# Sliding-window attention in rounds between the projections' blocks, stick-breaking attention one head per round

## The chip, the cores and the metric

One core of a Trainium2 chip runs the whole program. The metric is the device time of one execution in microseconds; the lower the better.

## What is computed

Two blocks on 512 tokens of width 1024. The first (gated delta net, differential attention, two SwiGLU layers) is not touched. In the second block the first mixer, `swa_sb_mixer`, projects the normalised rows into five parts: queries for 8 heads of 64 (qa), keys and values of 2 heads (ka, va), and queries, keys and values of 8 heads (qb, kb, vb).

- Sliding-window attention on qa, ka, va: q and k get an RMS norm and a rotation by position; each block of 128 queries sees its own 128 keys and the 128 before it, and a mask leaves the last 128 keys of each query. With s the scaled scores and a learned sink per head, m = max(max s, sink) and p = exp(s - m) / (sum exp(s - m) + exp(sink - m)); the output is p times va.
- Stick-breaking attention on qb, kb, vb: z = q k / 8 for the keys before the query; the weight of a key is exp(logsigmoid(z) - sum of softplus(z) over the keys between it and the query).

Both outputs side by side (1024 wide) are multiplied by `w_out` and added to x. Cross-attention to 256 memory rows, a convolutional FFN and a second layer follow.

## The kernel before, in words

Five programs, one per engine, are written out in full (`pe_program`, `act_program`, `dve_program`, `pool_program`, `sp_program`), and the order on an engine is the order in which its program issues. Each engine counts its instructions in one semaphore; a helper's `sig` gives an instruction a key, and `wait_ge(*K.at(key))` on another engine waits for it. `meet` (line 194) is a barrier of TensorE, VectorE, ScalarE and GpSimd. `bank` (line 213) hands out the eight PSUM banks in turn and waits until the former holder of a bank was read; `free` notes those reads.

Weights come in tiles of up to 2048 words. SyncE loads tile t once tile t - 2 was split; ScalarE makes the high part (fp32r), VectorE the low part, both inside `tile` (lines 352 and 314), one tile ahead of its use; TensorE waits for the low part. A projection multiplies with three fp32r matmuls for each product (`mm3`, line 232: lines 233, 234, 235). `mm` (line 229) is a plain matmul, here f32, `tr` (line 237) a transpose through the identity. In the trace an f32 `mm` leaves two records, an fp32r one or a `tr` one.

The stage that the change touches:

- `pe_ab_proj` (line 2505): projections of qa, of ka and va together, of qb, kb and vb, two weight tiles each. qa, ka/va and vb come out by tokens (`pe_proj_tok`, line 716: four banks are held over both tiles, 12 matmuls of each bank per tile), qb and kb by features (`pe_proj_feat`, line 699: one bank of 24 matmuls per 128 features). ScalarE copies the results out of PSUM; VectorE norms and rotates q and k in four steps (`dve_rotate`, line 2581), each with a square root on ScalarE in its middle. Last, 24 transposes turn q, k and a swapped copy of k.
- A barrier. Then sixteen sliding units, `SW_UNITS` (line 2628): block of 128 queries times a pair of heads, four in flight, started in turn by `pipeline` (line 404). Per unit: TensorE makes the scores; VectorE adds the mask, takes the maximum and subtracts it; ScalarE takes the exp; VectorE sums; TensorE transposes p (four transposes; two in block 0, which has no block before it), ScalarE copies it, TensorE makes the output, VectorE scales it (`pe_sw_unit`, `act_sw_unit`, `dve_sw_unit`, lines 2636 to 2714).
- A barrier. Then the eight heads of stick-breaking, two in flight (lines 2722 to 2808). Per head: scores in four banks (512, 384, 256 and 128 columns), scaled into z by VectorE; ScalarE takes abs, exp and ln of 1280 columns, with a table load ahead of ln and of the next exp; VectorE adds max(z, 0); GpSimd masks the four diagonal blocks; TensorE sums over the keys with a triangle and ones (`sb_after`); VectorE subtracts; ScalarE takes the exp; GpSimd masks again; TensorE makes the output; VectorE copies it. Both heads wait for the two before them.
- A barrier. Then eight turns of four transposes each give the output projection its features (`pe_ab_to_feat`, line 2811, with `act_to_feat` and `dve_to_feat` for the high and low parts), and `pe_cross` begins with that projection. GpSimd loads the memory rows here (`pool_cross_loads`).

Of the kernel before, what the change touches and what calls it, by code (L numbers as in the profile page):

```python
# [698 lines left out]
def pe_proj_feat(p, K, tag, src, hT, segs, ready=None):  # L699
    for c0 in range(0, src.shape[1], 256):  # L700
        m = p.tile((0, src[:, c0:c0 + 256]))
        w = K.wview(m, 256, 8)
        for f in range(2):
            for s, (o, n) in enumerate(segs):
                key = (tag, c0 // 128 + f, s)
                b = p.bank(*key)
                for k in range(8):
                    if ready and c0 + f + s == 0:
                        p.wait_ge(*K.at(*ready, k))
                    ins = p.mm3(b[:, 0:n], [x[:, k, f * 128:(f + 1) * 128] for x in w], [x[:, k, o:o + n] for x in hT],  # L710
                                k == 0, k == 7)
                ins.then_inc(*p.sig(key, ("used", m)))
                p.close(*key)


def pe_proj_tok(p, K, tag, src, hT, tiles, ready=None):
    n = src.shape[1]
    bs = [p.bank(tag, t) for t in tiles]
    for kh in range(2):
# [12 lines left out]
        if not kh:  # L732
            ins.then_inc(*p.sig(("used", m)))
# [1697 lines left out]


def act_to_feat(a, K, tag):
    for n, k, o, w in feat_order(4):
        a.wait_ge(*K.at(tag, n))
        a.cp(K.H5[0][:, k, :], K.ps(tag, n)[:, :]).then_inc(*a.sig((tag + "_hi", n)))


def dve_to_feat(v, K, tag):
    for n, k, o, w in feat_order(4):  # L2440
        v.wait_ge(*K.at(tag + "_hi", n))
        v.lo([x[:, k, :] for x in K.H5], K.ps(tag, n)[:, :]).then_inc(*v.sig((tag + "_lo", k)))
        v.free(tag, n)


# [46 lines left out]
def swapped_k(K):  # L2492
    return K.mem(SWW + 1600, 512).rearrange("p (t n) -> p t n", n=128)
# [10 lines left out]

def pe_ab_proj(p, K):
# [5 lines left out]
    pe_proj_feat(p, K, "ab_kb", wi[:, 1280:1792], K.H5, [(0, 512)])  # L2511
    pe_proj_tok(p, K, "ab_vb", wi[:, 1792:2304], K.H5, t4)
# [7 lines left out]


def act_ab_proj(a, K):
    qk, q5, k5, va, qb5, kb5, vb = ab_mem(K)
    cs, gr, snk, posi, posf, ang, kk, sn, co = ab_small(K)
    a.tile()
    a.tile()
    for i, dst in enumerate((sn, co)):
# [11 lines left out]
    for tag, dst, t0 in (("ab_qb", qb5, 0), ("ab_kb", kb5, 2)):  # L2539
        for j in range(2):  # L2540
            a.tile()
            for f in (2 * j, 2 * j + 1):
                a.wait_ge(*K.at(tag, f, 0))
                a.cp(dst[:, f, :], K.ps(tag, f, 0)[:, :]).then_inc(*a.sig())
                a.free(tag, f, 0)
            a.root(K.tmpc[:, 60:70], ("ab", t0 + j))
    a.tile()
    a.tile()
    for t in range(4):
        a.wait_ge(*K.at("ab_vb", t))  # L2550
        a.cp(vb[:, t, :], K.ps("ab_vb", t)[:, :]).then_inc(*a.sig())
        a.free("ab_vb", t)
# [53 lines left out]
def dve_ab_proj(v, K):  # L2606
# [3 lines left out]
    dve_angles(v, K)  # L2610
    dve_tok_out(v, K, "ab_q", range(4), lambda t: qk[:, t, 0:512])
    v.tile()
    v.tile()
    for t in range(4):
        v.tile()
        dve_rotate(v, K, t)
    v.tile()
    v.tile()
# [3 lines left out]
    for k in range(1, 6, 2):  # L2622
        v.wait_ge(*K.at("ab_T", k))
        v.cp(q5[:, k, :] if k < 4 else k5[:, k - 4, :], K.ps("ab_T", k)[:, :]).then_inc(*v.sig())
        v.free("ab_T", k)

# [4 lines left out]
def sw_mem(K, n):  # L2631
    j = n % 4
    return K.mem(SWW + 1600 + j * 1024, 512), K.mem(SWW + 2112 + j * 1024, 512), K.tmpc[:, j * 16:j * 16 + 16]


def pe_sw_unit(p, K, n, blk, hp):
    qk, q5, k5, va, qb5, kb5, vb = ab_mem(K)
    s, pt, c = sw_mem(K, n)
    size = 256 if blk else 128
    nb = size // 128  # L2640
    b = p.bank("sw_s", n)
    for u in range(2):
        h = hp + 2 * u
        half = h % 2
        kT, pr = k5[:, 0 if h // 4 == half else 1, :], slice(half * 64, half * 64 + 64)
        ins = p.mm(b[:, u * size:(u + 1) * size], q5[pr, h // 2, blk * 128:(blk + 1) * 128],
                   kT[pr, (blk + 1) * 128 - size:(blk + 1) * 128])
    ins.then_inc(*p.sig(("sw_s", n)))
    p.close("sw_s", n)
    yield  # L2650
    yield
    s3 = s[:, 0:2 * size].rearrange("p (u n) -> p u n", u=2)
    p.wait_ge(*K.at("sw_e", n))
    b = p.bank("sw_T", n)
    for u in range(2):
        for k in range(nb):
            ins = p.tr(b[:, (u * nb + k) * 128:(u * nb + k + 1) * 128], s3[:, u, k * 128:(k + 1) * 128])
    ins.then_inc(*p.sig(("sw_T", n)))
    p.close("sw_T", n)
    yield  # L2660
    p.wait_ge(*K.at("sw_p", n))
    b = p.bank("sw_o", n)
    for u in range(2):
        g = (hp + 2 * u) // 4
        for k in range(nb):
            ins = p.mm(b[:, u * 64:u * 64 + 64], pt[:, (u * nb + k) * 128:(u * nb + k + 1) * 128],
                       va[:, blk - nb + 1 + k, g * 64:g * 64 + 64], k == 0, k == nb - 1)
    ins.then_inc(*p.sig(("sw_o", n)))
    p.close("sw_o", n)


def act_sw_unit(a, K, n, blk, hp):
    s, pt, c = sw_mem(K, n)
    size = 256 if blk else 128
    s3 = s[:, 0:2 * size].rearrange("p (u n) -> p u n", u=2)
    yield
    a.wait_ge(*K.at("sw_d", n))
    a.act(s3, s3, ACT.Exp).then_inc(*a.sig())
    a.act(c[:, 2:4], c[:, 2:4], ACT.Exp).then_inc(*a.sig(("sw_e", n)))
    yield  # L2680
    a.wait_ge(*K.at("sw_T", n))
    if n >= 4:
        a.wait_ge(*K.at("sw_o", n - 4))
    a.cp(pt[:, 0:2 * size], K.ps("sw_T", n)[:, 0:2 * size]).then_inc(*a.sig(("sw_p", n)))
    a.free("sw_T", n)
    yield


def dve_sw_unit(v, K, n, blk, hp):
    cs, gr, snk = ab_small(K)[0:3]  # L2690
    s, pt, c = sw_mem(K, n)
    size = 256 if blk else 128
    s3 = s[:, 0:2 * size].rearrange("p (u n) -> p u n", u=2)
# [1522 lines left out]
```

## Time and profile before

| | |
|---|---|
| median of 3 runs | 4329.79 us (4325.04 to 4331.91) |
| the profiled execution, its time | 4329.3 us |
| its span, first to last instruction | 4327.5 us |
| mean granted TensorE clock | 0.937 |
| TensorE matmul busy | 3916.8 us, 91% |
| TensorE weight load busy | 3240.4 us, 75% |
| VectorE busy | 2124.9 us, 49% |
| ScalarE busy | 1587.7 us, 37% |
| GpSimd busy | 588.5 us, 14% |
| chain of waits, share of TensorE | 77% |

All times are of one profiled execution, from its first instruction on. The granted clock is a share of full speed: 1.00 is 2.4 GHz, 0.50 is 1.2 GHz. Matmuls overlap, so what one adds is the distance between starts and not the duration of one. A busy share says nothing of how fast the engine ran while busy.

### The profile page before, as it was taken

What the parts mean: (1) busy time and instruction counts of PE and PEld (TensorE: products, weight loads), DVE (VectorE), ACT (ScalarE), POOL (GpSimd) and SP (SyncE); (2) the same over time, 40 slices, a digit from 0 to 9 for tenths busy, and PEclk for the clock granted to TensorE, in tenths of its full rate; (3) what the DMA queues carried; (4) which work ended last, traced back from release to release, by engine and by line L of the source; (5) the groups of instructions that cost most, each with busy time, mean ns of one, the idle gap of its engine ahead of it and who ended that gap; (6) DMA issues with size and microseconds to landing.
All of it is one profiled execution on the core that took longest, in us unless ns stands there. A gap on an engine that the chain in (4) does not pass through costs nothing.

```text
span 4327.5 us, 67031 instructions
## 1 busy us (share of the span) xinstructions
PE 3916.8 (91%) x28034; PEld 3240.4 (75%) x28034; DVE 2124.9 (49%) x3061; ACT 1587.7 (37%) x2550; POOL 588.5 (14%) x692
## 2 busy tenths in 40 slices
PE   6988897878999988988899798898999998889999
PEld 4866786766888766856788586677888787677887
DVE  3545554656121453277423656454555427545564
ACT  3333333333111332164323334544334336544333
POOL 0035303532000001002100000200120003000220
PEclk8988898888999999999899895999999999899999
DMA  4234433131111121103122320141323230322322
GB/s 153 81 129 145 143 95 116 35 106 56 62 63 65 54 80 59 59 1 109 59 98 93 73 93 1 33 136 40 97 95 102 83 112 17 102 86 69 98 98 88
DMA packets 248532, 355.04 MB, mean 82 GB/s; under 512 B 9299, under 2 KB 158502, under 8 KB 247846
## 3 DMA queue, kind: packets, MB, share of 16 engines
q1 hardware_dynamic: 233840, 300.49, 21.5%
q0 software_dynamic: 13840, 50.11, 3.7%
q8 instruction: 220, 3.60, 0.4%
q14 instruction: 82, 0.67, 0.0%
q10 hardware_dynamic: 550, 0.17, 0.0%
HBM read 336.50 MB, written 14.24 MB: 81 GB/s over the span
## 4 chain that ended last, share of the span: by engine, by line
PE 77%; DVE 11%; ACT 6%; POOL 2%; issue 2%; DMA 1%; ACTq 0%; DVEq 0%; SPq 0%; POOLq 0%
PE psum L233 20%; PE psum L235 20%; PE psum L234 20%; PE psum L230 13%; ACT arena L341 3%; PE psum L239 3%; DVE arena L264 3%; DVE arena L274 2%; DVE rx L335 2%; POOL arena L379 1%; DVE rw L264 1%; DVE arena L278 1%; ACT arena L345 1%; ACT rw L345 1%; DVE arena L270 1%
## 5 line engine op out<-in xcount | busy, mean ns | idle before, releaser
L233 PE MATMUL psum<-rx,rw 128*128 128x512 f32 (+2 forms) x2768 | 1026.3, 371 | 47.0 <-DVE rx L335 29.1
L234 PE MATMUL psum<-rx,rw 128*128 128x512 f32 (+2 forms) x2768 | 1011.1, 365 | 0.0
L235 PE MATMUL psum<-rx,rw 128*128 128x512 f32 (+2 forms) x2768 | 1010.4, 365 | 0.0
L230 PE MATMUL psum<-arena 32*32 32x32 f32 (+10 forms) x13078 | 833.3, 260 | 173.7 <-ACT arena L345 59.7
L264 DVE TENSOR_TENSOR rw<-arena,rw 128x2048 fp32r<-128x2048 f32 (+2 forms) x239 | 538.5, 2253 | 862.5 <-ACT rw L345 857.4
L230 PEld LDWEIGHTS psum<-arena 32*32 32x32 f32 (+5 forms) x13078 | 649.1, 144 | 339.0 <-issue 108.4
L345 ACT ACTIVATE rw<-arena 128x2048 fp32r<-128x2048 f32 (+2 forms) x239 | 448.2, 1875 | 802.5 <-PE psum L235 780.6
L233 PE MATMUL psum<-rw,rx 128*128 128x512 f32 (+1 forms) x1720 | 676.7, 393 | 36.8 <-DVE rx L335 27.6
L234 PE MATMUL psum<-rw,rx 128*128 128x512 f32 (+1 forms) x1720 | 670.5, 390 | 0.0
L235 PE MATMUL psum<-rw,rx 128*128 128x512 f32 (+1 forms) x1720 | 670.3, 390 | 0.0
L233 PEld LDWEIGHTS psum<-rx,rw 128*128 128x128 f32 (+1 forms) x2768 | 530.8, 192 | 144.9 <-DVE rx L335 41.3
L379 POOL TENSOR_TENSOR arena<-arena 128x512 f32<-128x512 f32 (+5 forms) x364 | 446.7, 1227 | 1228.5 <-DVE arena L274 628.5
L345 ACT ACTIVATE arena<-psum 128x512 f32<-128x512 f32 (+6 forms) x675 | 313.9, 465 | 790.5 <-PE psum L235 438.5
L234 PEld LDWEIGHTS psum<-rx,rw 128*128 128x128 f32 (+1 forms) x2768 | 531.4, 192 | 84.2 <-issue 4.1
L235 PEld LDWEIGHTS psum<-rx,rw 128*128 128x128 f32 (+1 forms) x2768 | 530.7, 192 | 82.1 <-issue 0.3
L341 ACT ACTIVATE arena<-arena 128x512 f32<-128x512 f32 (+10 forms) x492 | 258.7, 526 | 501.1 <-DVE arena L274 219.8
L233 PEld LDWEIGHTS psum<-rw,rx 128*128 128x128 f32 x1720 | 325.4, 189 | 113.2 <-DVE rx L335 36.4
L274 DVE SCALAR_TENSOR_TENSOR arena<-arena 128x512 f32<-128x512 f32 (+7 forms) x465 | 351.9, 757 | 56.6 <-ACT arena L341 40.6
L235 PEld LDWEIGHTS psum<-rw,rx 128*128 128x128 f32 x1720 | 325.6, 189 | 67.4
L234 PEld LDWEIGHTS psum<-rw,rx 128*128 128x128 f32 x1720 | 325.8, 189 | 64.6
L239 PE MATMUL psum<-arena 128*128 128x128 f32 (+2 forms) x1300 | 212.9, 310 | 141.6 <-DVE arena L269 45.3
L264 DVE TENSOR_TENSOR arena<-arena,psum 128x512 f32<-128x512 f32 (+4 forms) x316 | 153.1, 484 | 308.6 <-PE psum L235 201.1
(71 smaller groups left out, 2068.7 us busy)
## 6 DMA issues: line engine op xcount, KB each, us to landing
arena<-in_ffn_w_up SPq DMA_DIRECT2D x66, 1024.0 KB, 5.1
arena<-in_ada_w SPq DMA_DIRECT2D x48, 1024.0 KB, 5.2
arena<-in_ffn_w_down SPq DMA_DIRECT2D x40, 1024.0 KB, 5.1
arena<-in_ffn_w_gate SPq DMA_DIRECT2D x22, 1024.0 KB, 5.1
arena<-in_dn_w_in SPq DMA_DIRECT2D x32, 512.0 KB, 5.3
arena<-in_xa_w_kv SPq DMA_DIRECT2D x16, 1024.0 KB, 5.0
arena<-in_hgrn_w_in SPq DMA_DIRECT2D x16, 1024.0 KB, 5.5
arena<-in_da_w_in SPq DMA_DIRECT2D x12, 1024.0 KB, 5.2
```

The source lines that it names most:

```text
L230: return self.e.matmul(out, l, r, start=start, stop=stop)
L233: self.e.matmul(out, l[0], r[0], start=start, stop=False)
L234: self.e.matmul(out, l[0], r[1], start=False, stop=False)
L235: return self.e.matmul(out, l[1], r[0], start=False, stop=stop)
L239: return self.e.transpose(out, a, self.K.ident[0:k, 0:k])
L264: return self.e.tensor_tensor(out, a, b, op)
L270: return self.e.tensor_scalar(out, a, s1, s2, op0, op1)
L274: return self.e.scalar_tensor_tensor(out=out, in0=a, scalar=s, in1=b, op0=op0, op1=op1)
L335: return self.e.tensor_tensor(dst[1], src, dst[0].bitcast(F32), SUB)
L341: return self.e.activation(out, a, f, **kw)
L345: return self.e.activation(out, a, ACT.Copy, **kw)
L379: return self.e.tensor_tensor(out, a, b, op)
```

## The change

- The sliding units are no longer a stage. `pe_proj_feat` and `pe_proj_tok` get a call `behind` after each block, and TensorE, ScalarE and VectorE go through 18 rounds: two behind each of the four kb blocks, one behind each of the eight half blocks of vb, two at the end. Round i has the scores of unit i, the output of unit i - 2 and the transposes of unit i - 1.
- The 24 transposes of q and k move from behind the vb projection to before the kb projection.
- The mask is added in PSUM by TensorE: a second, fp32r matmul of the identity with the mask, both copied once by ScalarE. The exp reads PSUM, with scale, with the negated maximum as its bias, and with its sum taken on the way; VectorE only takes the maximum and small columns.
- On ScalarE the square root of a rotation step comes before the eviction of the block, on VectorE two rotations follow each other between splits.
- Stick-breaking runs in ten rounds of one head, with z in four places and the softplus in two. Round i has the sums of head i - 1, the scores of head i + 1 and the output of head i - 2.
- The eight turns of the output are put into these rounds (rounds 1 to 4, 4, 6, 8 and 9).
- The three barriers go; GpSimd waits for the last head's output before it loads the memory rows.

```diff
-def pe_proj_feat(p, K, tag, src, hT, segs, ready=None):
+def pe_proj_feat(p, K, tag, src, hT, segs, ready=None, behind=None):
...
+            if behind:
+                behind(c0 // 128 + f)
...
 def pe_ab_proj(p, K):
...
     pe_proj_feat(p, K, "ab_qb", wi[:, 768:1280], K.H5, [(0, 512)])
-    pe_proj_feat(p, K, "ab_kb", wi[:, 1280:1792], K.H5, [(0, 512)])
-    pe_proj_tok(p, K, "ab_vb", wi[:, 1792:2304], K.H5, t4)
     p.wait_ge(*K.at("ab_ksw"))
     for k in range(6):
...
+    def behind(f):
+        for i in (2 * f, 2 * f + 1):
+            pe_sw(p, K, i)
+
+    pe_proj_feat(p, K, "ab_kb", wi[:, 1280:1792], K.H5, [(0, 512)], None, behind)
+    pe_proj_tok(p, K, "ab_vb", wi[:, 1792:2304], K.H5, t4, None, lambda kh, t: pe_sw(p, K, 8 + kh * 4 + t))
+    for i in (16, 17):
+        pe_sw(p, K, i)
...
 def dve_ab_proj(v, K):
...
     for t in range(4):
-        v.tile()
+        if t % 2 == 0:
+            v.tile()
         dve_rotate(v, K, t)
...
+    for i in range(18):
+        if i in (0, 4, 8, 12):
+            v.tile()
+        dve_sw(v, K, i)
...
+def pe_sw(p, K, i):
...
+            p.mm(b[:, u * size:(u + 1) * size], q5[pr, h // 2, blk * 128:(blk + 1) * 128],
+                 kT[pr, (blk + 1) * 128 - size:(blk + 1) * 128], True, False)
+            ins = p.mm(b[:, u * size:(u + 1) * size], one, mask[:, 256 - size:256], False, True)
+        ins.then_inc(*p.sig(("sw_s", i)))
+        p.close("sw_s", i)
+    if sw_unit(i - 2):
+        blk, hp = sw_unit(i - 2)
+        pt, nb = sw_mem(K, i - 2)[1], sw_size(i - 2) // 128
+        p.wait_ge(*K.at("sw_p", i - 2))
+        b = p.bank("sw_o", i - 2)
...
+    if sw_unit(i - 1):
+        e = sw_mem(K, i - 1)[0]
+        p.wait_ge(*K.at("sw_e", i - 1))
+        b = p.bank("sw_T", i - 1)
...
+def act_sw(a, K, i):
+    if sw_unit(i):
...
+            a.act(e[:, u * size:(u + 1) * size], K.ps("sw_s", i)[:, u * size:(u + 1) * size], ACT.Exp, scale=0.125,
+                  bias=bias[:, u:u + 1], accum_out=total[:, u:u + 1]).then_inc(*a.sig(("sw_e", i)))
+        a.free("sw_s", i)
+        a.act(sink, sink, ACT.Exp).then_inc(*a.sig(("sw_sum", i)))
+    if sw_unit(i - 1):
+        pt, n = sw_mem(K, i - 1)[1], 2 * sw_size(i - 1)
+        a.wait_ge(*K.at("sw_T", i - 1))
...
+        a.cp(pt[:, 0:n], K.ps("sw_T", i - 1)[:, 0:n]).then_inc(*a.sig(("sw_p", i - 1)))
...
+def dve_sw(v, K, i):
...
+        v.red(bias, r2(K.ps("sw_s", i)[:, 0:2 * sw_size(i)], 2), MAX).then_inc(*v.sig())
+        v.stt(bias, bias, -0.125, sinks(K)[:, hp:hp + 3:2], MUL, MIN).then_inc(*v.sig())
+        v.tt(sink, snk[:, hp:hp + 3:2], bias, ADD).then_inc(*v.sig(("sw_d", i)))
...
+def pe_sb(p, K):
...
+    sb_scores(p, K, 0)
+    for i in SB_ROUNDS:
+        if 0 <= i - 1 < 8:
+            h = i - 1
+            sp = sb_mem(K, h)[1]
+            p.wait_ge(*K.at("sb_fail", h))
...
+        if i + 1 < 8:
+            sb_scores(p, K, i + 1)
+        if 0 <= i - 2 < 8:
+            h = i - 2
+            z = sb_mem(K, h)[0]
+            p.wait_ge(*K.at("sb_a", h))
...
+        for k in sb_turns(i):
+            pe_ab_turn(p, K, k)
+
+def sb_turns(i):
+    return [k for k in range(8) if i == (k + 1 if k < 4 else min(2 * k - 4, 9))]
...
+def act_sb(a, K):
+    for i in SB_ROUNDS:
...
+            a.act(sp, sp, ACT.Ln, bias=1.0).then_inc(*a.sig(("sb_ln", i)))
+        if 0 <= i - 1 < 8:
+            z = sb_mem(K, i - 1)[0]
+            a.wait_ge(*K.at("sb_loga", i - 1))
+            a.act(z, z, ACT.Exp).then_inc(*a.sig(("sb_exp", i - 1)))
+        for k in sb_turns(i):
+            act_ab_hi(a, K, k)
...
+def pool_sb(g, K):
...
+            g.wait_ge(*K.at("sb_exp", i - 1))
+            for c0, size in CB:
+                g.tt(z[:, c0:c0 + 128], z[:, c0:c0 + 128], usm, MUL).then_inc(*g.sig(("sb_a", i - 1)))
+        if i < 8:
+            sp = sb_mem(K, i)[1]
+            g.wait_ge(*K.at("sb_sp", i))
+            for c0, size in CB:
+                g.tt(sp[:, c0:c0 + 128], sp[:, c0:c0 + 128], usm, MUL).then_inc(*g.sig(("sb_fail", i)))
...
+def pe_ab_turn(p, K, k):
+    if k < 4:
+        p.wait_ge(*K.at("sw_out", 15))
+    else:
+        p.wait_ge(*K.at("sb_out", 2 * k - 7))
...
     pe_ab_proj(p, K)
-    p.meet("ab_proj")
-    pipeline([pe_sw_unit(p, K, n, *u) for n, u in enumerate(SW_UNITS)], 4)
-    p.meet("sw")
-    pipeline([pe_sb_unit(p, K, h) for h in range(8)], 2)
-    p.meet("sb")
-    pe_ab_to_feat(p, K)
+    pe_sb(p, K)
...
     pool_ab_loads(g, K)
-    g.meet("ab_proj")
-    g.meet("sw")
-    pipeline([pool_sb_unit(g, K, h) for h in range(8)], 2)
-    g.meet("sb")
+    pool_sb(g, K)
+    g.wait_ge(*K.at("sb_o", 7))
     pool_cross_loads(g, K, 0)
```

## Rows read from the trace of the kernel before

**Rows 1.** Busy time by stretch: length, TensorE, weight load, VectorE, ScalarE, GpSimd, clock, DMA, GB/s
```profile
2600.00:2650.00 50.00, 49.72 (x165) 38.38 (x164) 41.04 (x105) 16.10 (x36) 0.00 (x0) 0.50 0.00 1
```

**Rows 2.** Chain of waits, 2440 to 2850: start us, us, engine, line, count
```profile
2483.93 5.34 PE psum L239 x32
...
2588.21 2.63 PE psum L239 x24
...
2617.65 1.04 PE psum L239 x4
2618.70 3.60 PE psum L230 x12
...
2661.93 5.24 PE psum L230 x8
...
2773.01 5.87 PE psum L239 x32
```

**Rows 3.** VectorE in order of time, the rotations and their surroundings
```profile
2527.89 0.82 DVE L264 TENSOR_TENSOR arena<-arena 128x640 f32<-128x640 f32 x1
...
2543.58 0.82 DVE L264 TENSOR_TENSOR arena<-arena 128x640 f32<-128x640 f32 x1
...
2550.95 2.29 DVE L264 TENSOR_TENSOR rw<-arena,rw 128x2048 fp32r<-128x2048 f32 x1
...
2581.69 0.62 DVE L290 COPY arena<-arena 128x256 f32<-128x256 f32 x2
```

**Rows 4.** ScalarE in order of time, the last eviction of qb
```profile
2544.72 0.60 ACT L345 ACTIVATE arena<-psum 128x512 f32<-128x512 f32 x1 [4.84 <-PE psum L235]
```

**Rows 5.** Busy time by stretches of 4 us, columns as in rows 1
```profile
2484.00:2488.00 4.00, 4.00 (x22) 4.00 (x23) 1.91 (x3) 2.50 (x4) 0.00 (x0) 0.58 0.74 25
...
2512.00:2516.00 4.00, 4.00 (x35) 4.00 (x35) 1.34 (x2) 0.53 (x1) 0.00 (x0) 1.00 0.24 65
...
2592.00:2596.00 4.00, 0.77 (x10) 0.57 (x8) 3.14 (x10) 1.15 (x1) 0.00 (x0) 1.00 0.00 0
...
2604.00:2608.00 4.00, 4.00 (x13) 2.96 (x12) 3.48 (x10) 1.00 (x3) 0.00 (x0) 0.50 0.00 0
...
2692.00:2696.00 4.00, 4.00 (x27) 3.28 (x26) 1.71 (x5) 2.39 (x2) 0.01 (x1) 1.00 0.00 0
...
2712.00:2716.00 4.00, 4.00 (x32) 3.83 (x31) 1.59 (x5) 1.27 (x1) 1.06 (x3) 1.00 0.00 0
```

**Rows 6.** Groups by shape in 2592 to 2662: busy us, mean ns, idle before
```profile
L278 DVE TENSOR_REDUCE arena<-arena 128x2 f32<-128x512 f32 x24 | 16.5, 686 | 1.7
...
L345 ACT ACTIVATE arena<-psum 128x512 f32<-128x512 f32 x12 | 7.2, 597 | 1.5 <-PE psum L239 0.5
...
L341 ACT ACTIVATE arena<-arena 128x256 f32<-128x256 f32 x4 | 1.7, 417 | 5.1 <-DVE arena L264 5.0
...
L341 ACT ACT_TABLE_LOAD x1 | 1.3, 1283 | 3.8 <-DVE arena L264 3.8
```

**Rows 7.** The four engines' orders of time in stick-breaking, 2660 to 2775
```profile
2676.20 21.05 PE L230 MATMUL psum<-arena 128*128 128x512 f32 x96 [6.49 <-POOL arena L379]
...
2684.27 1.27 ACT L341 ACTIVATE arena<-arena 128x1280 f32<-128x1280 f32 x1 [4.08 <-DVE arena L264]
...
2705.31 1.49 DVE L274 SCALAR_TENSOR_TENSOR arena<-arena 128x1280 f32<-128x1280 f32 x1 [5.05 <-ACT arena L341]
...
2716.87 2.29 DVE L269 TENSOR_SCALAR arena<-psum 128x512 f32<-128x512 f32 x4 [0.63 <-PE psum L230]
...
2758.41 2.05 POOL L379 TENSOR_TENSOR arena<-arena 128x128 f32<-128x128 f32 x4 [4.49 <-DVE arena L274]
...
2760.52 6.78 PE L230 MATMUL psum<-arena 128*128 128x512 f32 x40 [0.46 <-POOL arena L379]
...
2765.78 1.27 ACT L341 ACTIVATE arena<-arena 128x1280 f32<-128x1280 f32 x1 [3.78 <-DVE arena L264]
...
2769.23 3.26 PE L230 MATMUL psum<-arena 128*128 128x64 f32 x20 [1.93 <-POOL arena L379]
```

More of the change, by code:

```diff
@@ L713, in pe_proj_feat, with pe_proj_tok @@
                 p.close(*key)
-def pe_proj_tok(p, K, tag, src, hT, tiles, ready=None):
+            if behind:
+                behind(c0 // 128 + f)
+def pe_proj_tok(p, K, tag, src, hT, tiles, ready=None, behind=None):
     n = src.shape[1]
@@ L731, in pe_proj_tok @@
                 p.close(tag, t)
-        if not kh:
-            ins.then_inc(*p.sig(("used", m)))
+            elif t == tiles[-1]:
+                ins.then_inc(*p.sig(("used", m)))
+            if behind:
+                behind(kh, t)
 def out_chunks(Kn):
@@ L2538, in act_ab_proj @@
         a.free("ab_k", t)
-    for tag, dst, t0 in (("ab_qb", qb5, 0), ("ab_kb", kb5, 2)):
-        for j in range(2):
+    for f in range(4):
+        if f % 2 == 0:
             a.tile()
[L2542 to L2552, printed above, removed]
+        a.root(K.tmpc[:, 60:70], ("ab", f))
+        feat("ab_qb", qb5, f)
     for k in range(0, 6, 2):
         a.wait_ge(*K.at("ab_T", k))
-        a.cp(q5[:, k, :] if k < 4 else k5[:, k - 4, :], K.ps("ab_T", k)[:, :]).then_inc(*a.sig())
+        a.cp(q5[:, k, :] if k < 4 else k5[:, k - 4, :], K.ps("ab_T", k)[:, :]).then_inc(*a.sig("ab_T_a"))
         a.free("ab_T", k)
+    for f in range(4):
+        if f % 2 == 0:
+            a.tile()
+        feat("ab_kb", kb5, f)
+        for i in (2 * f, 2 * f + 1):
+            act_sw(a, K, i)
+    for kh in range(2):
+        a.tile()
+        for t in range(4):
+            if kh:
+                a.wait_ge(*K.at("ab_vb", t))
+                a.cp(vb[:, t, :], K.ps("ab_vb", t)[:, :]).then_inc(*a.sig("ab_vb_out"))
+                a.free("ab_vb", t)
+            act_sw(a, K, 8 + kh * 4 + t)
+    for i in (16, 17):
+        act_sw(a, K, i)
 def dve_angles(v, K):
@@ L2631, in sw_mem, with sinks, sw_mask @@
+def sinks(K):
+    return K.tmpc[:, 72:80]
+def sw_mask(K):
+    return K.rx[:, 8192:8320], K.rx[:, 8320:8576]
 def sw_mem(K, n):
     j = n % 4
-    return K.mem(SWW + 1600 + j * 1024, 512), K.mem(SWW + 2112 + j * 1024, 512), K.tmpc[:, j * 16:j * 16 + 16]
-def pe_sw_unit(p, K, n, blk, hp):
-    qk, q5, k5, va, qb5, kb5, vb = ab_mem(K)
[L2638 to L2669, printed above, removed]
```

279 lines of the change are left out of this document (140 added, 139 removed).

## The prediction

> **What bounds the kernel now.** The busy shares say that TensorE works 91% of the span, and the same holds in the two stages that the change touches, so I read its clock next. In the 50 us table one stretch of these stages has TensorE busy 49.72 of 50 us at a granted clock of 0.50 [rows 1]: full, and at half speed. The chain of waits [rows 2] gives the borders. The last projection ends at 2588.2; 24 transposes of q and k follow (2.63 us, 0.11 each, at full clock); the sixteen sliding units run until stick-breaking begins at 2661.93; the eight turns run from 2773.01 for 5.87 us, to 2778.88. A full unit (12 of 16) is 4 transposes and 12 matmul records, 1.04 + 3.60 = 4.64 us, back to back, on TensorE itself. An f32 matmul leaves two records, an fp32r one or a transpose one. The clock fell because TensorE did almost nothing in 2592 to 2596, and 13 records in 4 us did not raise it again [rows 5]. So sinking the units beside projections hides nothing from TensorE: both are its work. What it can win is the clock and gaps. Stick-breaking is different: TensorE waits there for POOL, and the next two heads cannot start before both heads are out.
>
> **Part 1, the projections.** The transposes move ahead of the kb projection, so they wait for the rotated q and k, which VectorE makes. Before, kb and vb covered that. The last qb eviction starts at 2544.72 [rows 4], so qb ends at 2544.65. On VectorE rotation 0 starts at 2527.89; rotation 1 starts at 2543.58 and the next operation at 2550.95, so a rotation without a stall is 7.3 us [rows 3]. The square root no longer stands behind an eviction, so all four take this: 4 x 7.3 = 29.2, one weight split 2.29 + 0.05 between them, and the swapped copies 0.7 [rows 3]. That gives 2527.89 + 32.2 = 2560.1. TensorE stands from 2544.65 to 2560.1, **15.5 us idle that is new**. ScalarE's order is no bound: its splits need only earlier weight tiles used. The negated sinks and the two mask copies lie before these waits beside the q projection and cost nothing; without that cover under 1 us.
>
> After such a gap the transposes start cold. In 2484 to 2488 a run of 32 transposes after a long idle had a mean clock of 0.58 [rows 5], and all 32 took 5.34 us [rows 2]: the rise came 3.4 us in. For 24 I take 3.4 us at 0.23 and 9 at 0.11, 4.4 us. The Trainium skill, page "TensorE: Matmul & The Clock Gate", Part 4, states that the clock gate does not open for transposes; here it opened inside a run of nothing else, so the measurement decides. By that rule the 24 would cost 6.2 us and the sum below come out 1.8 us later.
>
> Dense work left, kb and vb: 2588.2 - 2544.65 = 43.5 us.
>
> The sunk units: with no long idle beside them I take them at the full level. That the clock holds over such work is seen in 2692 to 2696 and 2712 to 2716, when only stick-breaking's half-height scores and 64-column outputs ran, at 1.00 [rows 5]. A full unit is half of 4.64, 2.3 us; the second of these windows gives 0.125 per record, 8 output records 1.0 us, which agrees. The mask adds two fp32r matmuls of 256 columns; the k projection has this shape, 35 in 4 us [rows 5], 0.11 each, so 0.23. 12 x 2.55 = 30.6; the four block-0 units have half of most of it, about 1.4, 5.6 together. **36 us.** Switching between f32 and fp32r inside one sum is seen nowhere; I take nothing, and a whole extra fp32r matmul (0.11) for each of 32 mask matmuls, 3.5 us, as the upper end.
>
> Waits in the rounds: between a unit's scores and its transposes lie the reduction 0.69 [rows 6], two small operations, two exps of 0.42 each (256 columns) and between that and the outputs a copy of 0.60 behind the next unit's exps [rows 6]. That is 2.9 us from scores to copied; TensorE has 2.2 to 2.5 us of its own between them in the two back-to-back rounds of a kb block, so 0.75 us is open in each of three blocks and 1.3 in the first; with a vb block of 2.7 us between rounds nothing is open; the two tail rounds leave 1.5 and 0.75. Sum 5.5. VectorE's own addition of the mask and subtraction of the maximum go as well; TensorE was the one waited for in nearly all full units, so this is counted at nothing. For clock dips I add 2 us.
>
> New end: 2560.1 + 4.4 + 43.5 + 36 + 5.5 + 2 = 2651.6, before 2661.9: **10.3 us won**.
>
> **Part 2, stick-breaking.** Follow one head per round. In round i POOL first masks the outputs of head i-1 (after its last exp), then the softplus of head i; TensorE sums head i after both; VectorE subtracts; ScalarE takes the exp. That is a loop: exp of head i-1, POOL 2.05, POOL 2.05, TensorE's sums to exp start 5.26 (2760.52 to 2765.78, warm), exp 1.27 [rows 7], hand-overs 0.25: 10.9 us. Beside it, ScalarE's three passes and two table loads (1.28 each [rows 6]) reach the exp's table load at 10 us in rounds with a turn, so 11 us. VectorE has 2.29 for the next scores, 1.49 for the softplus [rows 7], as much as 2.3 for the subtractions and a small copy, 6.5 us; TensorE 4.5 + 2.2 + 2.2 to 2.5 + a turn of 0.45, 9.4 us: neither is the bound while warm. TensorE idles about 1.5 us a round.
>
> Opening: scores and their eviction 2.6, three passes and a table 5.1, softplus 1.5, POOL 2.05, then the sums cold, as 2676.20 to 2684.27 = 8.07 us, and the exp 1.27 [rows 7]: 20.8 with hand-overs. Seven rounds of 11: 77. Head 1 starts cold after a 3.7 us gap too, and once more for another: 3. Tail: POOL 2.1, outputs between 2.2 and 3.3 us [rows 7], copy 0.5, one turn, and the first dense work cold: 7.2. Sum 108. Before: 2778.88 - 2661.93 = 117. **9 us won**, seven of the eight turns (5.87 us in all before) inside the rounds included.
>
> Moved past queues: POOL's memory load now waits for the last outputs and is issued about 1 us before the output projection instead of 5 us; its rows are turned only after two weight chunks, over 20 us in, so 4 us later costs nothing; if they were late, up to 4 us. The weight queue on SyncE sees the same tiles in the same order, earlier. The barriers between the stages go; what they held is held by the data waits above.
>
> **Sum.** 10.3 + 9 = 19.3 us off the profiled execution's 4329.3 us (span 4327.5): **4310 us**. The median of the runs, 4329.79, is the same within 0.5 us.
>
> **Rivals.** About 0.2% (9 us) is what a measurement of this kernel can tell, so faster is below 4321 and slower above 4338.
>
> (a) Slower: the clock falls in the sunk rounds. For: the same operations, busy 4.00 of 4 us, held 0.50 from 2596 on [rows 1, 5]; the stretch before them would now be 15.5 us idle, and kb's pairs have waits. Against: dense blocks of 2.7 and 5.4 us stand between, and rows at 1.00 show light work holding the clock. Price: 12 x 5.1 + 4 x 3 = 73 instead of 36, so 4347; with half of the dense work cold too, 4369. It decides against the change once over half of the sunk units run at the low level (19 of 37 us). Chance 0.15.
>
> (b) The 1.5 us idle of each stick-breaking round is enough to lose the clock. For: in the last head 1.93 us idle between outputs was followed by 20 records in 3.26 us, slower than 0.125 each [rows 7]. Against: dense sums follow at once. Price: 8.07 - 5.26 = 2.8 us for seven heads, 20, of which 3 are counted: 4327, or 4318 if in half of them. Chance 0.17.
>
> (c) It does not do what it says: the sunk units win nothing, since the new idle of 15.5 us and longer waits eat the clock's gain; only part 2 is left: 4320 to 4325. Chance 0.08.
>
> (d) Better: no waits in the rounds and no dips, 7.5 us less, and one cold start fewer: 4300. Chance 0.10.
>
> The forecast, 4302 to 4320: 0.50.
>
> **Numbers.** Faster: 0.50 + 0.10 + a third of (b), 0.66. Slower: (a), 0.15. The same: the rest, 0.19. The range must leave out no more than 0.2: from 4294, below (d) by the bounds of the waits, to 4337, which takes in (b) and (c) and leaves (a).
>
> **What would show it.** TensorE idle of about 15 us just before the q and k transposes, ended by VectorE; then clock 1.00 in the stretches of kb and vb with 36 to 40 us more work in them; mask matmuls near 0.11 us; first scores of stick-breaking near 2652; rounds of 11 us; projection start near 2760. I am wrong in part 1 if the clock in these stretches is below 0.9 or the idle over 20 us, and in part 2 if rounds exceed 12 us.

## The result and the profile after

The changed kernel takes 4340.37 us (median of 16 runs), the kernel before 4331.38 us beside it: ratio 1.0020, 95% interval 1.0012 to 1.0028. It is slower by about 9 us where 19 us less was forecast. The profiled execution has a time of 4339.06 us and a span of 4337.2 us, against 4327.5 before; the mean granted clock is 0.940 against 0.937. TensorE is busy 3911.5 us against 3916.8. What precedes the touched stages is 0.8 us late, and the output projection starts at 2787.25 instead of 2778.64: 7.8 of the 9.7 us of span arise in the touched stages and 1.1 behind them.

TensorE of the kernel after, in order of time (start, duration, engine, line, operation, output from input, count, idle before and what ended it). The first two lines answer to the 24 transposes of [rows 2], the 2619.87 group is one full round between two half blocks of vb, and the rest is the last rounds and stick-breaking:

```profile
2560.90 5.38 PE L239 MATMUL psum<-arena 128*128 128x128 f32 x24 [15.44 <-DVE arena L290]
2565.93 0.78 PE L233 MATMUL psum<-rx,rw 128*128 128x512 f32 x1
...
2619.87 0.70 PE L230 MATMUL psum<-arena 64*128 64x256 f32 x2
2620.50 0.39 PE L230 MATMUL psum<-rx 128*128 128x256 f32 x1
2620.81 0.70 PE L230 MATMUL psum<-arena 64*128 64x256 f32 x2
2621.44 0.38 PE L230 MATMUL psum<-rx 128*128 128x256 f32 x1
2621.66 1.00 PE L230 MATMUL psum<-arena 128*128 128x64 f32 x8
2622.49 0.61 PE L239 MATMUL psum<-arena 128*128 128x128 f32 x4
2622.86 0.47 PE L233 MATMUL psum<-rw,rx 128*128 128x512 f32 x1
...
2664.25 1.10 PE L230 MATMUL psum<-arena 128*128 128x64 f32 x8 [2.01 <-ACT arena L345]
...
2666.53 9.69 PE L230 MATMUL psum<-arena 128*128 128x64 f32 x24 [0.69 <-ACT arena L345]
...
2696.09 11.13 PE L230 MATMUL psum<-arena 128*128 128x512 f32 x48 [4.33 <-POOL arena L379]
...
2708.89 9.33 PE L230 MATMUL psum<-arena 128*128 128x512 f32 x48 [1.24 <-POOL arena L379]
...
2720.58 10.83 PE L230 MATMUL psum<-arena 128*128 128x512 f32 x48 [1.92 <-POOL arena L379]
...
2745.47 12.02 PE L230 MATMUL psum<-arena 128*128 128x512 f32 x48 [3.05 <-POOL arena L379]
...
2787.25 0.78 PE L233 MATMUL psum<-rw,rx 128*128 128x512 f32 x1
```

The reader is to see four things. The new idle of 15.44 us, ended by VectorE, is there as forecast. A full round is the six groups from 2619.87 to the start of the next projection matmul at 2622.86, **2.99 us**. The last group with outputs begins at 2666.53 and the first scores of stick-breaking some 0.95 us later, at about 2667.5; before it was 2661.93. And a head's 48 records take 9.33 us in a warm round and up to 12.02 us in others. Stick-breaking to the output projection is 2667.5 to 2787.25, 119.8 us, where before had 116.7 (2661.93 to 2778.64).

The same kernel, busy time and granted clock by stretches (columns as in [rows 1]):

```profile
2540.00:2560.00 20.00, 5.45 (x25) 4.17 (x23) 18.39 (x32) 2.40 (x5) 0.00 (x0) 0.74 0.16 52
...
2564.00:2565.00 1.00, 1.00 (x6) 1.00 (x5) 0.39 (x1) 0.35 (x1) 0.00 (x0) 0.50 0.00 0
...
2566.00:2567.00 1.00, 1.00 (x5) 0.85 (x4) 0.68 (x1) 0.91 (x2) 0.00 (x0) 0.68 0.00 0
...
2600.00:2620.00 20.00, 19.86 (x98) 14.49 (x97) 7.19 (x19) 7.83 (x20) 0.00 (x0) 0.98 0.07 23
...
2640.00:2644.00 4.00, 4.00 (x19) 3.21 (x18) 2.85 (x7) 1.19 (x5) 0.00 (x0) 0.72 0.42 103
...
2744.00:2748.00 4.00, 2.53 (x4) 1.20 (x5) 0.00 (x0) 3.89 (x4) 1.25 (x3) 0.52 0.00 0
```

The clock does hold in the sunk rounds (0.98; [rows 1] had 0.50), with dips such as 2640 to 2644, and it drops in stick-breaking behind waits of 1.9 to 4.9 us, where those of 1.24 us and less left it at 1.00.

GpSimd of the kernel after, in order of time:

```profile
2704.50 4.34 POOL L379 TENSOR_TENSOR arena<-arena 128x128 f32<-128x128 f32 x8 [8.47 <-ACT arena L341]
2716.26 4.27 POOL L379 TENSOR_TENSOR arena<-arena 128x128 f32<-128x128 f32 x8 [7.42 <-ACT arena L341]
2728.70 4.34 POOL L379 TENSOR_TENSOR arena<-arena 128x128 f32<-128x128 f32 x8 [8.17 <-ACT arena L341]
```

GpSimd's starts mark the rounds: from 2691.78 to 2766.53 six rounds, 12.5 us each. Before, two heads took 25.9 us (2674.10, 2700.34, 2725.95 and 2751.87 are GpSimd's first groups of the four pairs there), 13.0 a head. The chain of waits of the kernel after, from one round's sums on (start, us, what):

```profile
2696.09 11.13 PE psum L230 x48
2707.22 0.46 PE psum L239 x4
...
2707.69 0.61 ACT rx L345
...
2708.38 1.28 ACT arena L341
...
2709.68 1.27 ACT arena L341
2710.97 1.28 ACT L341
2712.27 1.28 ACT arena L341
...
2713.61 1.28 ACT L341
2714.91 1.28 ACT arena L341
...
2720.58 10.83 PE psum L230 x48
```

It holds, one after the other: all 48 records of TensorE's round, the turn (2707.22), ScalarE's high part of that turn (2707.69), which stands in ScalarE's program ahead of the next head's passes, three passes, two table loads and an exp, 4.3 us of GpSimd (2716.26 above), and only then TensorE's next sums. From 2696.09 to 2720.58 are 24.5 us, for two rounds.

### The profile page after: what moved, and what is told of

It reads as the page before. It is cut to its first block, busy times and chain, and to the rows that moved or that the text cites. A ratio compares the mean times of both kernels' runs of the same rounds, so it can differ in the third digit from the quotient of the medians.

```text
span 4337.2 us, 67048 instructions
## 1 busy us (share of the span) xinstructions
PE 3911.5 (90%) x28066; PEld 3228.4 (74%) x28066; DVE 2093.8 (48%) x3014; ACT 1597.2 (37%) x2600; POOL 587.7 (14%) x692
## 4 chain that ended last, share of the span: by engine, by line
PE 76%; DVE 11%; ACT 7%; POOL 2%; issue 2%; DMA 1%; ACTq 0%; DVEq 0%; SPq 0%; POOLq 0%
PE psum L233 20%; PE psum L235 20%; PE psum L234 20%; PE psum L230 13%; ACT arena L341 3%; DVE arena L264 3%; PE psum L239 3%; DVE arena L274 2%; POOL arena L379 2%; DVE rx L335 1%; DVE rw L264 1%; ACT arena L345 1%; DVE arena L278 1%; ACT rw L345 1%; DVE arena L270 1%
## 5 line engine op out<-in xcount | busy, mean ns | idle before, releaser
L233 PE MATMUL psum<-rx,rw 128*128 128x512 f32 (+2 forms) x2768 | 1026.0, 371 | 47.8 <-DVE rx L335 29.7
L230 PE MATMUL psum<-arena 32*32 32x32 f32 (+9 forms) x13078 | 826.6, 259 | 179.2 <-ACT arena L345 66.5
L230 PEld LDWEIGHTS psum<-arena 32*32 32x32 f32 (+5 forms) x13078 | 639.0, 144 | 349.8 <-issue 107.9
L341 ACT ACTIVATE arena<-arena 128x512 f32<-128x512 f32 (+11 forms) x476 | 249.4, 524 | 476.0 <-DVE arena L274 220.9
L274 DVE SCALAR_TENSOR_TENSOR arena<-arena 128x512 f32<-128x512 f32 (+8 forms) x481 | 354.5, 737 | 39.2 <-ACT arena L341 21.9
```

The costliest lines, as they stand in the source:

```text
L230: return self.e.matmul(out, l, r, start=start, stop=stop)
L233: self.e.matmul(out, l[0], r[0], start=start, stop=False)
L274: return self.e.scalar_tensor_tensor(out=out, in0=a, scalar=s, in1=b, op0=op0, op1=op1)
L341: return self.e.activation(out, a, f, **kw)
```

## The experiments

Each ratio is to the kernel before, timed on the same chip beside it, with its 95% interval. Two changed kernels are compared by their ratios, and with intervals of 0.1 to 0.15% to each side a difference below 0.2% (9 us) between them is at the edge of what the times settle. The profile is of one execution, which can lie up to 12 us off the median; lengths between two events of one trace are used where that matters.

**sw_alone and sb_alone: each half by itself.** The first has the change's projections with sunk units, then before's stick-breaking and turns; the second the reverse.

```diff
 # sw_alone
-    pe_sb(p, K)
+    p.meet("sw")
+    pipeline([pe_sb_unit(p, K, h) for h in range(8)], 2)
+    p.meet("sb")
+    pe_ab_to_feat(p, K)
...
 # sb_alone
-    pipeline([pe_sb_unit(p, K, h) for h in range(8)], 2)
-    p.meet("sb")
-    pe_ab_to_feat(p, K)
+    pe_sb(p, K)
```

> The change's sliding part alone; stick-breaking and the eight turns as before, behind a barrier. Theory: the sunk part by itself costs about 5 us (new TensorE idle 15.4 us before the q and k transposes, and a full unit takes 3.23 us at full clock where 2.55 was forecast), so 4336 us against 4331 before. Rival: the two parts harm each other (the stage hands TensorE over cold to rounds that never warm it), then this one alone is at or below the time before, 4331 or less.

> The change's stick-breaking part alone, with the turns in its rounds; projections and sliding units as before. Theory: rounds of about 12.4 us (11 were forecast), from the loop through GpSimd's two maskings and from TensorE starting the sums at a low clock; 4 to 6 us slower than before, 4336. Rival: if the forecast's sum holds for this part by itself, 9 us faster, 4322.

sw_alone: 4337.34 us, 1.0013 (1.0004 to 1.0022). sb_alone: 4332.95 us, 1.0010 (1.0001 to 1.0018), rounds 12.4 us. So neither half wins; the losses, 5.6 and 4.3 us by the ratios, add up to about the 9 of both. Both forecast wins, 10.3 and 9 us, are wrong.

The trace of sw_alone also shows how much the clock varies with the same instructions. TensorE in order of time, and a stretch:

```profile
2563.94 4.47 PE L239 MATMUL psum<-arena 128*128 128x128 f32 x24 [15.44 <-DVE arena L290]
```

```profile
2567.00:2568.00 1.00, 1.00 (x9) 1.00 (x9) 0.42 (x1) 0.40 (x1) 0.00 (x0) 0.83 0.00 0
```

Behind the same idle the 24 transposes took 4.23 us here (to 2568.17), with the clock rising inside them, and 5.03 us in the changed kernel. From their start to the last group with outputs are 110.2 us at a mean clock of 0.89 here and in act_later, 105.6 to 105.7 us at 0.94 in the changed kernel, pool_swap and fill: 4.5 us for the clock alone.

**t_late: the transposes behind the kb projection.** VectorE gets the time of kb for its rotations; the units then go two by two behind each half block of vb.

```diff
+    pe_proj_feat(p, K, "ab_kb", wi[:, 1280:1792], K.H5, [(0, 512)])
     p.wait_ge(*K.at("ab_ksw"))
     for k in range(6):
...
-    def behind(f):
-        for i in (2 * f, 2 * f + 1):
+    def behind(kh, t):
+        for i in (8 * kh + 2 * t, 8 * kh + 2 * t + 1):
             pe_sw(p, K, i)
```

> The changed kernel with the q and k transposes behind the kb projection instead of before it, and two sliding rounds behind each half block of vb. Theory: the idle of 15.4 us and the cold start of the transposes (5.0 against 2.6 us) and of the first kb block go, about 3 us of waits in the paired rounds come: 14 to 18 us below the changed kernel, 4324. Rival: VectorE's rotations hold the stage however the work is ordered and the sunk rounds wait longer, so less than 6 us is won.

4323.38 us, 0.9979 (0.9970 to 0.9988), 0.41% below the changed kernel (18 us). The stretch 2540 to 2560, busy time:

```profile
2540.00:2560.00 20.00, 19.78 (x88) 16.05 (x87) 18.45 (x28) 5.95 (x9) 0.00 (x0) 1.00 0.34 105
```

TensorE is now busy 19.78 of 20 us where it was 5.45. The outputs of the last units begin at 2649.48 instead of 2666.53, 17.05 us earlier: the idle of 15.44, and some of what its cold start cost (the transposes took 5.03 us in the changed kernel).

**pool_swap: GpSimd masks the softplus of head i ahead of the outputs of head i - 1.**

```diff
 def pool_sb(g, K):
     for i in SB_ROUNDS:
+        if i < 8:
+            sp = sb_mem(K, i)[1]
+            g.wait_ge(*K.at("sb_sp", i))
...
         if 0 <= i - 1 < 8:
             z = sb_mem(K, i - 1)[0]
             g.wait_ge(*K.at("sb_exp", i - 1))
...
-        if i < 8:
-            sp = sb_mem(K, i)[1]
-            g.wait_ge(*K.at("sb_sp", i))
...
```

> The changed kernel with one order turned round: in each stick-breaking round GpSimd masks the softplus of head i first and the outputs of head i-1 second. Theory: the loop exp, masking, masking, sums, exp is cut; a round becomes bound by TensorE at 9.8 us and TensorE does not idle, so its clock stays up: 12.5 to about 10 us for each of seven rounds, 15 to 20 us below the changed kernel, 4323. Rival: ScalarE's order (the high part of a turn, which waits for TensorE, ahead of the next head's passes) sets the rounds; then they stay above 11.5 us and less than 8 us is won.

4321.14 us, 0.9981 (0.9972 to 0.9989). GpSimd in order of time:

```profile
2690.13 4.26 POOL L379 TENSOR_TENSOR arena<-arena 128x128 f32<-128x128 f32 x8 [8.74 <-DVE arena L274]
2700.65 4.26 POOL L379 TENSOR_TENSOR arena<-arena 128x128 f32<-128x128 f32 x8 [6.27 <-DVE arena L274]
2711.00 4.26 POOL L379 TENSOR_TENSOR arena<-arena 128x128 f32<-128x128 f32 x8 [6.08 <-DVE arena L274]
```

The rounds fall to 10.1 us (2690.13 to 2720.50 is three). The releaser names the reason: GpSimd waits for VectorE's softplus sum, and no longer for ScalarE's exp (2704.50 after). The order of two masks was worth the whole forecast win of part 2 and more.

**fill: two needless dense matmuls at the end of each of eight rounds.** It tells whether the gaps cost clock.

```diff
+        if i < 8:
+            b = p.bank("fill", i)
+            for _ in range(2):
+                p.mm(b[:, 0:512], K.ones, qb5[:, 0, :])
+            p.close("fill", i)
```

> The changed kernel with two needless 128x512 f32 matmuls into a spare bank at the end of each of the first eight stick-breaking rounds on TensorE, 1.7 us at full clock each round. Theory (the low clock after TensorE's gaps of 3 to 5 us is what makes rounds 12.4 instead of 11.3 us): the sums start warm, most rounds near 11.3, about 5 us won although 14 us of work are added: 4334. Rival (the order of the engines alone sets the rounds): no gain, or up to 8 us slower, 4340 to 4348.

4331.41 us, 1.0000 (0.9991 to 1.0009): 0.2% below the changed kernel although TensorE has more to do (busy 66.5 us in 2700 to 2770, instead of 57.7). Its clock there is 1.00 instead of 0.91, and a round takes 11.6 us (2690.62 to 2771.94 is seven). By themselves needless matmuls can only add time, so at least 0.9 us of the change's 12.5 is clock lost in the gaps.

**act_later: a turn's two copies moved into the next round**, ScalarE's behind ln, VectorE's behind the softplus sum.

```diff
             a.act(sp, sp, ACT.Ln, bias=1.0).then_inc(*a.sig(("sb_ln", i)))
+        for k in sb_turns(i - 1):
+            act_ab_hi(a, K, k)
...
             a.act(z, z, ACT.Exp).then_inc(*a.sig(("sb_exp", i - 1)))
-        for k in sb_turns(i):
-            act_ab_hi(a, K, k)
```

> The changed kernel with ScalarE's high part of a turn (and VectorE's low part) moved into the next round, behind ln and the softplus sum. Theory: in the chain the turn's high part stands between TensorE's turn and the next head's passes, and only so two rounds close into one loop of 24.4 us; without it a round is GpSimd 4.3 + sums 5.3 to 6.9 + exp 1.3, 10.9 to 12.4 us: 3 to 8 us won, 4335. Rival: GpSimd's order alone holds the rounds, 12.4 us as before, same as the changed kernel, 4340.

4351.02 us, 1.0044 (1.0029 to 1.0059), a miss: 10 us slower than the changed kernel, where a win was expected. TensorE in order of time:

```profile
2715.61 4.44 PE L230 MATMUL psum<-arena 64*128 64x128 f32 x22 [0.95 <-DVE rx L335]
```

Inside each round TensorE stands for VectorE's low part (L335): the turn's bank is read late, and the banks are handed out in turn, so the next scores wait for it. The same wait stands in four rounds (0.95 us, once 1.73), a round takes 14.1 us (GpSimd's groups at 2714.55 and 2756.98 are three apart), and the clock of the whole stage is 0.74 instead of 0.80. In this trace 6.4 us of the loss lie in stick-breaking and 4.5 in the sliding stretch, which the edit does not touch (see sw_alone). The copy was moved off one loop into another.

**mask_dve: the mask added by VectorE again**, in the rounds (the exp then reads SBUF).

```diff
-                 kT[pr, (blk + 1) * 128 - size:(blk + 1) * 128], True, False)
-            ins = p.mm(b[:, u * size:(u + 1) * size], one, mask[:, 256 - size:256], False, True)
...
+        v.stt(e3, r2(K.ps("sw_s", i)[:, 0:2 * size], 2), 0.125, bcm(ab_small(K)[0][:, 256 - size:256], 2), MUL,
+              ADD).then_inc(*v.sig())
```

> The changed kernel with the mask added by VectorE again, in the rounds: one more VectorE pass per unit (scale and mask from PSUM to SBUF), no mask matmuls. Theory: the mask matmuls hold TensorE 0.53 us per full unit (0.31 + 0.22, and the f32 scores beside them take 0.31 per record instead of 0.21), so a full unit falls from 3.23 to 2.7 us or less; 8 us less TensorE time, 2 to 3 us more waits in the paired rounds: 5 us below the changed kernel, 4334. Rival: VectorE's pass only lengthens the way from scores to exps and the rounds wait as much longer: no difference.

4340.38 us, 1.0020 (1.0009 to 1.0030), the same as the change; the rival held. TensorE in order of time:

```profile
2622.90 2.16 PE L230 MATMUL psum<-arena 64*128 64x256 f32 x12
...
2628.21 1.13 PE L230 MATMUL psum<-arena 64*128 64x256 f32 x4
```

A round with its vb half block is 5.31 us instead of 5.91 (2622.90 to 2628.21; 2619.87 to 2625.78), so two mask matmuls cost 0.60 us. But the waits grow: in the first three kb pairs they were 0.55, 0.59 and 0.59 us and are 2.43, 1.67 and 2.00, and from the transposes to the last outputs they sum to 13.8 us instead of 6.4.

**late_swap: the edits of t_late and pool_swap together.**

> Both mended orders together: transposes of q and k behind kb with two rounds per half block of vb, and GpSimd's softplus masking first. Measured alone they gave 17 and 18 us off the changed kernel's 4340. Theory: they lie in different stretches and add: 4305. Rival: one takes the other's gain (a colder hand-over between the parts): 4312 or more.

4301.93 us, 0.9933 (0.9918 to 0.9948): **29 us faster than before**, 38 faster than the change. The two repairs, 0.41% and 0.39% below the change, add up within the noise. The next four were made from this kernel.

**no_mask: the 32 mask matmuls left out**, and nothing in their place: the scores stay unmasked.

```diff
-            ins = p.mm(b[:, u * size:(u + 1) * size], one, mask[:, 256 - size:256], False, True)
```

> late_swap without its 32 mask matmuls (the mask is left out of the scores, nothing else changes). Theory, from the trace of the changed kernel: a full unit's two mask matmuls cost 0.53 us of TensorE and a block-0 unit's about 0.3, so 12 x 0.53 + 4 x 0.3 = 7.6 us go: ratio to the kernel before 0.9933 - 0.0018 = 0.9915, about 4294. Rival: the waits of each round grow by what the matmuls took, as they did with the mask on VectorE, and the time stays near 0.993 (4302).

4299.67 us, 0.9935 (0.9922 to 0.9948): the times show no difference to late_swap, though their intervals are as wide as the 7.6 us looked for. TensorE in order of time:

```profile
2625.90 2.16 PE L230 MATMUL psum<-arena 64*128 64x256 f32 x12
2627.90 0.61 PE L239 MATMUL psum<-arena 128*128 128x128 f32 x4
2628.44 1.13 PE L230 MATMUL psum<-arena 64*128 64x256 f32 x4
2630.32 1.10 PE L230 MATMUL psum<-arena 128*128 128x64 f32 x8 [0.76 <-ACT arena L345]
```

The first round of a pair is 2.54 us (2625.90 to 2628.44); in late_swap it is 3.16 (2612.86 to 2616.02), again 0.6 us for two masks. A wait of 0.76 us or more now stands in each of the eight pairs, where late_swap has one in four of them. The two traces can be added up from the transposes' start to the last outputs: units 35.6 instead of 47.8 us, waits 12.4 instead of 6.0, dense work 1.4 more, in all 77.4 instead of 81.8 us. So the rival held in part: waits take back over half of what the masks cost on TensorE, and some 4 us may be left, which the times neither show nor exclude.

**combo: late_swap with the edit of mask_dve.**

> late_swap with the mask added by VectorE, its result in SBUF for the exp. Theory: the first round of each pair still waits for VectorE's longer way (reduction plus addition), so that what TensorE saves (7.6 us) comes back as waits, as in the kernel with the mask on VectorE alone: no difference to late_swap, 0.993 (4302), within 3 us. Rival: with two rounds per vb half block and full clock there is slack for it, and it wins 5 to 7 us: 0.9918 (4295).

4312.35 us, 0.9959 (0.9946 to 0.9973), a miss: 11 us slower than late_swap. TensorE in order of time:

```profile
2615.36 1.10 PE L230 MATMUL psum<-arena 128*128 128x64 f32 x8 [1.55 <-ACT arena L345]
...
2617.34 0.63 PE L234 MATMUL psum<-rw,rx 128*128 128x512 f32 x1
...
2626.56 1.77 PE L230 MATMUL psum<-arena 128*128 128x64 f32 x8 [1.70 <-ACT arena L345]
2628.12 1.06 PE L239 MATMUL psum<-arena 128*128 128x128 f32 x4
```

Waits of 1.55 us and more come back in every pair (3.61 in the first), and behind them the projection's matmuls run at the low level (0.43 apart from 2617.34 on, where 0.23 is the full level). The profiled execution is the slowest of five (4324.04 us) and late_swap's its fastest (4294.85), so only lengths inside the stage are compared: from the transposes to the last outputs 91.5 us at a clock of 0.81 instead of 81.8 at 0.95. The units take 7.9 us less (39.9), the waits 10.6 more (16.6) and the dense work 7.3 more (32.8). So the mask on TensorE is right, though not because it is cheap there: it shortens VectorE's way while TensorE would wait.

**turns_end: all eight turns behind the last round.**

```diff
-    return [k for k in range(8) if i == (k + 1 if k < 4 else min(2 * k - 4, 9))]
+    return list(range(8)) if i == 9 else []
```

> late_swap with all eight turns behind the last round of stick-breaking instead of inside the rounds. Theory: a turn in a round is cover that costs little, now that GpSimd releases the sums first, so taking seven of them out of the rounds gives back at most 7 x 0.2 us, and standing in a row behind the last round they cost about 5.2 us more at the end: 0.9942 (4306). Rival: each turn lies in the loop with 0.46 us of TensorE and 0.61 us of ScalarE, so the rounds fall from 10.15 to about 9.1 us, which pays for the end: 0.993 (4301 to 4302) or lower.

4299.57 us, 0.9936 (0.9924 to 0.9949): no difference to late_swap. The interval holds the theory's 0.9942 and the rival's 0.993 alike; the rounds decide. TensorE in order of time:

```profile
2672.45 54.17 PE L230 MATMUL psum<-arena 128*128 128x512 f32 x280 [2.06 <-POOL arena L379]
...
2742.62 5.97 PE L239 MATMUL psum<-arena 128*128 128x128 f32 x32
```

For 54 us TensorE has no gap, and a round takes 9.2 us (GpSimd's groups at 2690.05 and 2726.84 are four rounds apart): that is TensorE's own time, the floor. late_swap's round is 10.2 us (2688.06 to 2729.03 is four), so the rival's mechanism held: a turn costs about 1 us in a round, and what this wins the turns in a row take back for the most part (5.7 us, 2742.62 to 2748.34; from the last sliding outputs to the projection 102.7 us instead of 105.1). Without pool_swap this was not tried.

**rounds_row: the 18 sliding rounds in a row behind the vb projection**, same instructions.

```diff
-    pe_proj_tok(p, K, "ab_vb", wi[:, 1792:2304], K.H5, t4, None, behind)
-    for i in (16, 17):
+    pe_proj_tok(p, K, "ab_vb", wi[:, 1792:2304], K.H5, t4)
+    for i in range(18):
         pe_sw(p, K, i)
```

> late_swap with the 18 sliding rounds in a row behind the vb projection instead of beside its half blocks: same instructions. Theory (sinking hides nothing of TensorE's own work, it fills waits): each of some 12 full rounds waits about 0.6 to 1.0 us for the exps where before every second one did, 5 to 8 us more, at full clock: 0.9950 (4309). Rival: with waits in every round the clock falls to its low level as in the kernel before, and the 37 us of units take 20 us or more longer: 0.998 (4322) or above.

4322.03 us, 0.9987 (0.9979 to 0.9996): 23 us slower than late_swap by the ratios; the rival held. TensorE in order of time, and then stretches (columns as in [rows 1]):

```profile
2593.70 1.11 PE L230 MATMUL psum<-arena 128*128 128x64 f32 x4 [0.27 <-ACT arena L345]
...
2608.12 1.22 PE L230 MATMUL psum<-arena 64*128 64x256 f32 x2
2609.27 0.58 PE L230 MATMUL psum<-rx 128*128 128x256 f32 x1
...
2613.89 1.22 PE L230 MATMUL psum<-arena 64*128 64x256 f32 x2
```

```profile
2592.00:2596.00 4.00, 3.73 (x16) 2.70 (x15) 1.37 (x6) 3.00 (x12) 0.00 (x0) 0.71 0.00 0
...
2600.00:2660.00 60.00, 60.00 (x186) 40.32 (x186) 17.91 (x66) 20.24 (x65) 0.00 (x0) 0.50 0.00 1
```

The waits were 0.55 and 0.27 us, then none until the tail, yet the clock fell and stayed at 0.50 through 60 us in which TensorE was busy without a gap. From the transposes to the last outputs are 106.4 us at a mean clock of 0.64, where late_swap has 81.8 at 0.95, with waits of 2.4 us against 6.0. A round takes 5.77 us (2608.12 to 2613.89), twice the 2.99. What sinking wins is the full clock that the dense blocks beside the rounds keep. The Trainium skill, "TensorE: Matmul & The Clock Gate", section "Loop structure matters more than you think", says matmuls stay warm when the loop keeps them back to back; here these did not (0.50 at 60.00 us busy of 60), so the measurement decides against reading it that way for such small f32 matmuls. What in them does it was not tried.

## Why the prediction was wrong

The direction was wrong: two gains of about 10 us were forecast, and each was a loss of 4 to 6 us. Its steps, one by one:

- **Idle before the transposes.** 15.5 forecast, 15.44 measured, ended by VectorE. Right.
- **The transposes cold.** 4.4 forecast, 5.03 measured in the changed kernel, 4.23 in sw_alone. In the changed kernel all 24 ran at the low level (0.21 apart; the stretch 2564 to 2565 is at 0.50, 2566 to 2567 at 0.68), and the rise came with the projection's matmuls behind them. The forecast had it inside, as in [rows 5]. The rule of the Trainium skill that was set against it ("TensorE: Matmul & The Clock Gate", Part 4: the gate does not open for transposes) would have given 6.2 us for them, at the 0.26 of the cold units in [rows 2]; at the 0.23 of the forecast itself it is 5.5. The changed kernel's trace fits that rule in that none of the 24 ran faster. The 32 of before do not, nor do the same 24 in sw_alone, which stood at 0.83 in their fourth microsecond: there the clock rose with transposes alone, so the measurements decide against the rule. Which of the two comes differs between the profiled executions (5.03 also in pool_swap, fill and mask_dve, 4.24 in act_later), and no run shows why.
- **The sunk units, the term that failed in part 1.** 36 forecast. From 2565.93 to 2667.5 are 101.6 us: 48.8 in projections, 6.4 in waits, and 46.4 in the units. A full round is 2.99 us beside a vb half block and 3.28 in pairs, not 2.55: the two mask matmuls take 0.31 and 0.22 by their starts, 0.53 instead of 0.23. That is above the upper end of the bound, which allowed 0.11 more for each. Taken away, they give back 0.60 (mask_dve), so what they do to the f32 matmuls beside them counts too; a round without them is 2.36 us before its vb block, as the forecast had it (2.3). Over 12 full units that is 4.4 of the 10.4 us; 0.8 is one round at a dipped clock (3.81 us, from 2639.64). The other 5 lie in the block-0 units and in the rounds in pairs, 6.55 us for two (2604.48 to 2611.03), and no run takes them apart.
- **Dense work and dips.** 43.5 and 2 forecast, 48.8 measured. **Waits**, 5.5 forecast (its terms add to 5.8), 6.4 measured. The sizes agree, the places only in part: 1.97 us stand at 2639.64, beside a vb block, where nothing was said to be open; TensorE waits there for the copy of a vb bank, which ScalarE makes behind a weight split of 1.91 us. The kb pairs had 0.55 to 0.59, the tail 2.01 and 0.69.
- The sum of part 1, 2651.6 plus 0.8 of earlier delay, became 2667.5: 10.4 us from the units, 3.3 from dense work, 0.9 from waits, 0.6 from the transposes. Against before, 15.5 us idle ate what the clock gave. Rival (c), winning nothing, came nearest; the clock rival (a) did not come in the changed kernel (0.94 over the stretch), while rounds_row shows the same rounds at 0.50 for 60 us.
- **Stick-breaking rounds, the term that failed in part 2.** 11 forecast, 12.5 measured, over the 12 that was named as the sign of being wrong. Two steps did it. "That is a loop: exp of head i-1, POOL 2.05, POOL 2.05, TensorE's sums to exp start" follows the data, and ScalarE's order stood "beside it". In the chain after they are in series: a turn's high part on ScalarE waits for the end of TensorE's round and holds up the next head's passes, and the softplus mask, which releases the sums, stands on GpSimd behind the exp of the head before. pool_swap shows the GpSimd step by itself: with ScalarE's order left as it was the rounds fall to 10.1 us. That ScalarE's order alone would have cost anything is not shown, since act_later moved its copy into another wait. And the waits of 1.9 to 4.9 us that the loop leaves cost clock, rival (b), shown by fill. Three of the six rounds were partly cold (10.8 to 12.0 instead of 9.33). Stick-breaking to the projection became 119.8 us where the sum had 108.
- **The turns for free inside the rounds.** Forecast as the 5.9 us won with seven rounds of 11. turns_end shows no gain: about 1 us each in the loop.
- **GpSimd's memory load** came at 2786.42, 0.8 us before the projection; the rows wait is hidden, as forecast.

The range, 4294 to 4337, missed the 4340 by 3 us: it took rival (b), 4327, and rival (c), 4320 to 4325, each by itself. Here both came together, and part 1 lost where (c) had it win nothing.

## What to carry to other kernels

Work that is sunk beside dense matmuls is worth the clock that the dense blocks keep, 23 us here against the same rounds in a row, but only if nothing new stands before it: ask first which engine makes its inputs and put the consumer late enough for it, 17 us here. In a software pipeline of rounds follow each engine's program order and not the data alone: one engine that serves an older item ahead of a newer one can put its whole round on the chain, and exchanging two groups of GpSimd gave 17 us. Two mishaps of a kernel can come together, so the range should hold their sum.

## What was not expected of the hardware

- Small f32 matmuls in a row (64x256, 128x64, with 128x128 transposes) held the low level for 60 us at 60.00 us busy in rounds_row; between dense blocks the same instructions ran at 0.95 to 1.00.
- An fp32r matmul of 256 columns, 0.11 apart in a run of its kind [rows 5], took 0.31 and 0.22 between f32 matmuls, and two of them cost a round 0.60 us.
- The same 24 transposes behind the same idle of 15.44 us took 5.03 us in the changed kernel and 4.23 in sw_alone, and the stretch from their start to the last sliding outputs 105.6 and 110.2 us, with the same instructions in it.
- Needless matmuls in a stage with gaps made the kernel 0.2% faster (fill).
- Taking 12 us of TensorE's units away shortened the stretch by only 4.4 us in the traces, and the times by nothing that they can tell (no_mask), since VectorE's and ScalarE's way to the transposes and outputs then sets the pairs.
